# Step sizes of a state-space mixer on 96 partitions, three half blocks of the output projection moved, inputs loaded first

## The chip, the cores and the metric

The kernel runs on one core of a Trainium2 chip, in one launch. The metric is the device time of one execution in microseconds (us). TensorE (PE) multiplies, VectorE (DVE), ScalarE (ACT) and GpSimd (POOL) do the rest, SyncE (SP) and POOL issue the transfers (DMA) from and to HBM. All data is float32; a matrix product of 128 x 128 by 128 x 384 shows as two PE instructions in the trace.

## The reference, cut to what matters

One layer of a trunk over 128 context tokens and 256 latent tokens, width 2048. The layer's modulation is SiLU(cond) @ w_ada + b_ada, six columns of 2048. A mixer sub-layer projects the normed tokens by w_in and splits into two groups: a Mamba-2 state-space group (SSD, 16 heads of 64, state 128, chunks of 128 tokens, both directions) and an RWKV-7 group (16 heads of 64, both directions). Their outputs, 1024 channels each, are concatenated and go through w_out (2048 x 2048). Then 16 SwiGLU experts, each on its top tokens, and a final norm.

The step sizes of the SSD group:

```python
dt = softplus(dt_raw.reshape(b, seq, 2, 16) + dt_bias)     # 2 directions, 16 heads
A = -exp(A_log)
a_cum = cumsum(dt * A, axis=chunk)                         # within chunks of 128 tokens
decay_in = exp(where(lower, a_cum[i] - a_cum[j], -inf))    # backward direction: reversed tokens
decay_to_end = exp(a_cum[last] - a_cum)
chunk_decay = exp(a_cum[last])
y_off = (C * exp(a_cum)) @ h_in
y = y_f + reverse(y_b) + D * x
```

and at the end of the mixer `x += gate_m * (concat(y_ssd, y_rwkv) @ w_out)`.

## The kernel before

Channels lie on partitions and the 384 tokens (3 tiles of 128, the first of them the context) along the free axis. Stages follow each other, each a block in which every engine has its own list of instructions in a fixed order; engines meet by semaphores only. At the end of a block all engines wait for each other.

**setup** (lines 187 to 342). SP loads the constant table (L219), some twenty small parameter arrays as rows of 128 (L211), x in three tiles of 1 MB (L237, L239), the position table (L240), and then sixteen 1 MB pieces of w_ada through a ring of eight (L216), the narrow columns of w_in and three blocks of it. TensorE transposes the parameter rows (L270), then x (L279), then multiplies eight strips of w_ada, sums the squares for the norm, and multiplies the other eight strips (L258).

**ssd_shared** (L382 to L684) computes what all heads share. TensorE goes through sixteen more strips of w_ada (L483, ring of four) between products of w_in, then projections 3, 4 and 5 (L455), x and z of the first pair of heads (L520), B's tokens and the product of B and C (L525, L528), and last the transposes of three row arrays (L536). The raw step sizes come out of projection -1 on partitions 96 to 127; two products with slices of the identity (L460) bring both directions onto 16 partitions, one per head, with tile `dt` of 16 x 2 x 384. DVE computes the softplus by a series (L627 to L639), the running sums by a scan over 384 tokens with a reset mask (L643), their reversal for the backward direction (L647 to L653), then the four convolutions of B and C (L347 to L661) with sigmoids on ACT, the lora mixing (L671 to L674), and the product of step size and decay (L679), for which it waits for ACT's exponentials (L601 to L603). SP loads the per-head scalars A_log, dt_bias and D first of all in this block (L413 to L415).

**ssd_heads** (L687 to L945) goes over 8 pairs of heads. SP first writes the running sums, their exponentials and seven per-head values to HBM (L760), and reads them back spread over partitions: for each pair four running-sum rows onto 128 partitions each (`spread_sums`, L749), two loads of decays and two of the seven values onto 64 partitions each (`spread_decays`, L756, L757). In a turn SP issues, in this order: the z weight of the next pair (from the second turn on), the spread sums once the masks of this pair are made (`M_seg`), the x weight of the pair after once its x projection is done (L739), the final states, the next states, and the spread decays. TensorE (`body`, L801) places the 32 products of the next pair's x and z (L797, 16 each) between eight strips of w_ada (L812), which POOL loads through a ring of four (L717), and the products of the pair itself. DVE makes the masks (L907), 12 instructions of 128 x 128 from the spread sums and a column of `tokq`.

**rwkv** (L984 to L1690), 8 pairs again. In the last two pairs the free places of TensorE take products of the first half of w_out (k from 0 to 7) for output blocks 0 to 11 (L1177), which DVE adds to x (L1595). At the end stand, for the last pair, mean (L1189), centring (L1565, L1570), square, variance (L1189), root, reciprocal and scaling (L1574 to L1584). hT, the normed tokens, is last read some pairs earlier; its room is free by then.

**project_out** (L1706 to L1836) goes over 16 output blocks of 128 channels: blocks 0 to 11 with k from 8 to 15, blocks 12 to 15 with all 16 (L1770), from a ring of four weights and into three banks. DVE adds each block to x (L1825), and `done` (L1755) multiplies it by the router's weights (L1758) and transposes it (L1762). Between the blocks stand the gate columns (L1776) and the router's shift (L1782). Block n waits for the addition of block n - 3. DVE builds the router's weights (L1819, L1820) before its first addition.

**experts** (from L1843) streams the experts' weights through a ring.

## Time and profile before

| | us |
|---|---|
| median of 3 runs | 2345.91 (2338.87 to 2346.77) |
| the profiled execution | 2347.66 |
| its span | 2345.7 |
| setup, to the first work of the next stage | 70.9 |
| ssd_shared, to TensorE's first strip of the pair stage | 214.1 |
| ssd_heads, to TensorE's first RWKV product | 484.8 |
| rwkv and project_out, to TensorE's first expert-stage work | 1342.7 |
| experts, to the end | 2345.7 |

| engine | busy us | share of the span |
|---|---|---|
| PE | 2134.6 | 91% |
| PE weight load | 1072.5 | 46% |
| DVE | 854.1 | 36% |
| ACT | 399.7 | 17% |
| POOL | 156.9 | 7% |

The shares are means over stages with different limits. In a timeline a row gives the start, the time to the end of the last of its instructions, the engine, the line, and in brackets how long the engine was idle before it and what ended that. "SPq" rows are transfers as SP issues them, not their landing.

### The profile page before, as it was taken

The page shows a single profiled execution, that of the slowest core. Times are in us where ns is not written, and L with a number is a line of the kernel's source. Part 1 is how long each engine was busy: PE and PEld are TensorE (multiplying, and loading weights), DVE is VectorE, ACT ScalarE, POOL GpSimd, SP SyncE. Part 2 cuts the span into 40 slices and gives each one's busy share as a digit, 9 for nine tenths or more (in the row PEclk, how much of TensorE's full clock was granted, in tenths as well). Part 3 has the DMA queues.
Part 4 walks back from the last instruction along what each step waited for, and adds up shares of the span by engine and source line. Part 5 has one row for each costly group of instructions (what it writes and reads, how often), then busy time and mean ns, then how long its engine had stood idle before and what let it go on. Part 6 is the DMA issues. An engine that isn't in the chain of part 4 may idle for free. (4 is left out here: it accounts for less than half of the span.)

```text
span 2345.7 us, 38339 instructions
## 1 busy us (share of the span) xinstructions
PE 2134.6 (91%) x16420; PEld 1072.5 (46%) x16420; DVE 854.1 (36%) x1835; ACT 399.7 (17%) x807; POOL 156.9 (7%) x186
## 2 busy tenths in 40 slices
PE   5897999999999999999979889989988999899886
PEld 2354555446666666666655443324322432243222
DVE  1245434434566666656431131112111211122113
ACT  1123122212332233222101110001000100010002
POOL 0000111100011011101101100000000000000000
PEclk9898999999999999999989989999999999999998
DMA  9954999942211111111123399999999999999996
GB/s 368 355 167 132 316 353 339 323 128 67 52 49 43 42 52 48 43 42 40 39 76 104 124 371 413 413 414 412 413 413 413 413 413 413 413 413 413 413 413 263
DMA packets 271121, 594.03 MB, mean 253 GB/s; under 512 B 25853, under 2 KB 166231, under 8 KB 249847
## 3 DMA queue, kind: packets, MB, share of 16 engines
q1 hardware_dynamic: 253559, 524.64, 60.0%
q0 software_dynamic: 17408, 67.11, 7.5%
q8 instruction: 124, 2.03, 0.4%
q14 instruction: 30, 0.25, 0.0%
HBM read 586.89 MB, written 4.82 MB: 252 GB/s over the span
## 5 line engine op out<-in xcount | busy, mean ns | idle before, releaser
L1985 PE MATMUL bank<-w_early,picked 128*64 128x512 f32 x1024 | 242.3, 617 | 44.7 <-DMA w_early<-exp_w_up 42.6
L1184 PE MATMUL bank<-arena,w_rkv 128*128 128x384 f32 x736 | 271.7, 502 | 4.4 <-ACT raw_rkv L1408 4.4
L2164 DVE TENSOR_TENSOR x_sum<-x_sum,bank 128x512 f32<-128x512 f32 x180 | 115.4, 684 | 319.6 <-PE bank L1965 319.6
L2009 PE MATMUL bank<-arena,hid 128*64 128x512 f32 x768 | 173.5, 600 | 13.1 <-issue 11.3
L1985 PE MATMUL bank<-arena,picked 128*64 128x512 f32 x768 | 175.4, 598 | 5.2 <-DMA arena<-exp_w_up 4.8
L1184 PEld LDWEIGHTS bank<-arena,w_rkv 128*128 128x128 f32 x736 | 130.1, 189 | 89.7 <-issue 17.4
L1985 PEld LDWEIGHTS bank<-w_early,picked 128*64 128x64 f32 x1024 | 77.6, 141 | 201.2 <-issue 200.9
L797 PE MATMUL bank<-arena,w_xz 128*128 128x384 f32 x448 | 157.0, 499 | 2.6 <-DMA w_xz<-w_in 2.6
L2051 ACT COPY gu<-bank 112x512 f32<-112x512 f32 x32 | 17.2, 589 | 660.7 <-PE bank L1985 660.7
L1156 POOL TENSOR_TENSOR WI<-WX,cst 128x384 f32<-128x384 f32 x80 | 80.6, 1023 | 594.7 <-DVE WX L1613 385.7
L797 PEld LDWEIGHTS bank<-arena,w_xz 128*128 128x128 f32 x448 | 82.3, 191 | 82.3 <-issue 31.0
L1770 PE MATMUL bank<-arena,w_out_ring 128*128 128x384 f32 x320 | 108.0, 493 | 11.5 <-DMA w_out_ring<-w_out 11.5
L1985 PEld LDWEIGHTS bank<-arena,picked 128*64 128x64 f32 x768 | 54.1, 136 | 119.8 <-issue 119.4
L1965 PE MATMUL bank<-outs,G 48*128 48x512 f32 x384 | 107.0, 638 | 1.4 <-DVE outs L2183 1.4
L2009 PEld LDWEIGHTS bank<-arena,hid 128*64 128x64 f32 x768 | 60.9, 138 | 103.6 <-issue 101.6
L2183 DVE TENSOR_TENSOR outs<-bank,gates 128x512 f32<-128x512 f32 x32 | 20.6, 686 | 237.6 <-PE bank L2009 237.6
L1640 DVE TENSOR_TENSOR WI<-WI,bank 128x384 f32<-128x384 f32 x80 | 44.1, 551 | 130.4 <-PE bank L1320 85.7
L1177 PE MATMUL bank<-arena,w_rkv 128*128 128x384 f32 x192 | 76.7, 525 | 8.6 <-DVE arena L1595 8.6
L1770 PEld LDWEIGHTS bank<-arena,w_out_ring 128*128 128x128 f32 x320 | 60.5, 193 | 51.4 <-DMA w_out_ring<-w_out 12.1
L812 PE MATMUL bank<-w_ada,cond 128*32 128x512 f32 x512 | 66.1, 623 | 8.6 <-DMA w_ada<-w_ada 4.0
L1307 PEld LDWEIGHTS bank<-WI 64*64 64x64 f32 x1920 | 60.5, 136 | 27.1 <-issue 27.1
L2095 POOL TENSOR_TENSOR arena<-x_sum,gfin 128x512 f32<-128x512 f32 x4 | 5.0, 1276 | 983.6 <-DVE x_sum L2164 983.6
(405 smaller groups left out, 2732.3 us busy)
## 6 DMA issues: line engine op xcount, KB each, us to landing
arena<-exp_w_down SPq DMA_DIRECT2D x96, 1024.0 KB, 18.9
w_ada<-w_ada POOLq DMA_DIRECT2D x64, 1024.0 KB, 8.0
w_early<-exp_w_gate SPq DMA_DIRECT2D x64, 1024.0 KB, 18.6
w_early<-exp_w_up SPq DMA_DIRECT2D x64, 1024.0 KB, 18.8
arena<-exp_w_gate SPq DMA_DIRECT2D x48, 1024.0 KB, 19.0
arena<-exp_w_up SPq DMA_DIRECT2D x48, 1024.0 KB, 18.7
w_ada<-w_ada SPq DMA_DIRECT2D x32, 1024.0 KB, 11.8
w_exp<-exp_w_down SPq DMA_DIRECT2D x32, 1024.0 KB, 23.8
```

What stands on the lines that cost most here:

```text
L797: mm = pe.matmul(ps[j][:, 0:T], w[:, j, k], hT[:, k], start=(k == 0), stop=(k == KC - 1))
L812: mm = pe.matmul(ps[4][32 * j:32 * j + 32, :], cond[:, 2 * n + j // 2], wa[:, n % AR, j // 2, j % 2 * 512:(j % 2 + 1) * 512], start=(n == ...
L1156: nc.gpsimd.tensor_tensor(CT[d], W2[d][:, :, 2], m, ALU.mult).then_inc(S(f"CT_ready{d}"), 1)
L1177: mm = pe.matmul(ps[6][:, 0:T], w[:, m % 3, n % 8], mixed[:, n % 8], start=(n % 8 == 0), stop=(n % 8 == 7))
L1184: mm = pe.matmul(ps[feed_bank(i)][:, 0:T], spare[:, n] if first else w[:, m % 3, n % 8], hT[:, n % KC], start=(n % KC == 0), stop=(n % KC ...
L1307: mm = pe.matmul(ps[3 * d][HP[1 - h], c * Q:(c + 1) * Q], CT[d][HP[h], c], X[d][HP[h], c], start=True, stop=True)
L1640: ins = V.tensor_tensor(X[d], X[d], c6(ps[3 * d + 1][:, 0:T]), ALU.subtract)
L1770: mm = pe.matmul(ps[n % BANKS][:, 0:T], w[:, n % RING, k], mixed[:, k], start=(k == first(n)), stop=(k == KC - 1))
L1965: pe.matmul(ps[bank + h][:], G[rows, t * P:(t + 1) * P], outs[rows, b], start=True, stop=True).then_inc(S("add_in"), 1)
L1985: mm = pe.matmul(ps[b][COLS[j], :], picked[:, k, at:at + 64], halves[j][:, c * 1024 + b * 512:c * 1024 + (b + 1) * 512], start=(k == 0), s ...
L2009: mm = pe.matmul(ps[4 + b][COLS[j], :], hid[:, f], wd[:, n * 512:(n + 1) * 512], start=(f == 0), stop=(f == 7))
L2164: V.tensor_tensor(y, y if e else x, ps[(LAST_BANKS[i // 2 % 4] if e == LAST else 6) + i % 2][:], ALU.add).then_inc(S("added"), 1)
```

## The change

Three edits.

1. In setup, the three loads of x and the position table are issued right after the constants, ahead of the small rows.
2. In the shared stage, the step sizes lie on 96 partitions (3 tiles x 2 directions x 16 heads) by 128 tokens. Three products (one per tile) select them; every step of the series works on 96 x 128; the scan needs no reset mask; `back` marks the backward rows, for which the running sum is (a + total) - sum. The per-head scalars are loaded once per tile, after the first four pieces of w_ada. ACT's exponentials come before the convolutions, and DVE's product too. The row arrays are transposed by three products, and the per-head values (totals' exponentials and D) reach all partitions by products of ones with diagonals into tile `whole`, in place of the HBM round trip. TensorE does this ahead of x and z; B's tokens stand between x, and the halves of z. SP writes the sums and exponentials to HBM and spreads the first pair's within this stage. In HBM they lie as 96 rows of 128, so each spread copy reads three pieces (two for the decays) of 128 values.
3. The second halves of w_out's output blocks 0, 1 and 2 are loaded into hT's room at the end of the RWKV stage; seven of their eight products (k from 8 to 14) run there, around mean and variance of the last pair, and stay in banks 0 to 2. project_out does only k = 15 for them; its loads begin with block 3, and `done` of blocks 0 to 2 follows block 3.

```diff
             at = CONST["row"][0]
             sp.dma_start(cst[:], table[:, 0:at]).then_inc(S("cst_in"), 16)
+            sp.dma_start(xtok[:, 0, :], I["x_prompt"][0]).then_inc(S("x_in"), 16)
+            for t in range(2):
+                sp.dma_start(xtok[:, 1 + t, :], I["x_sample"][0, t * P:(t + 1) * P, :]).then_inc(S("x_in"), 16)
+            sp.dma_start(grid[:], table[:, at:]).then_inc(S("grid_in"), 16)
             rows_in(0, 0, I["b_ada"].rearrange("l (r c) -> (l r) c", c=P))
...
+def spread_sums(sp, S, d_cum, seg, c):
+    rows = d_cum.rearrange("(t d h) c -> h d t c", t=TILES, d=2)
+    for u in range(4):
+        h = 2 * c + u // 2
+        sp.dma_start(seg[:, u].rearrange("p (t c) -> p t c", t=TILES), rows[h:h + 1, u % 2].to_broadcast([P, TILES, P])).then_inc(S("seg_in"), 16)
+
+def spread_decays(sp, S, d_ea, eac, c):
+    rows = d_ea.rearrange("(t d h) c -> h d t c", t=TILES, d=2)
+    for h in range(2):
+        for d in range(2):
+            dst = eac[h * HD:(h + 1) * HD, d].rearrange("p (t c) -> p t c", t=2)
+            sp.dma_start(dst, rows[2 * c + h:2 * c + h + 1, d, 1:TILES].to_broadcast([HD, 2, P])).then_inc(S("eac_in"), 16)
...
+                    for t in range(TILES):
+                        rows = slice(t * 2 * HEADS, (t + 1) * 2 * HEADS)
+                        sp.dma_start(small[rows, 0:1], I["ssd_A_log"].rearrange("l d h -> (d h) l")).then_inc(S("small_in"), 16)
+                        sp.dma_start(small[rows, 1:2], I["ssd_dt_bias"].rearrange("l d h -> (d h) l")).then_inc(S("small_in"), 16)
+                    sp.dma_start(d_col[:], I["ssd_D"].rearrange("l h -> h l")).then_inc(S("small_in"), 16)
...
             for n in range(KC):
+                if n == AR:
+                    load_scalars()
...
             sp.wait_ge(S("bc_proj"), 1)
             sp.dma_start(w_xz[:, 1], w_in[:, :, 0:P]).then_inc(S("wz_loaded"), 16)
+            sp.wait_ge(S("sums_ready"), 1)
+            sp.dma_start(d_cum, cum[:, 1]).then_inc(S("rows_out"), 16)
+            sp.wait_ge(S("decay_exp"), 1)
+            sp.dma_start(d_ea, ea[:]).then_inc(S("rows_out"), 16)
+            sp.wait_ge(S("rows_out"), 32)
+            spread_sums(sp, S, d_cum, seg, 0)
+            spread_decays(sp, S, d_ea, eac, 0)
             sp.wait_ge(S("x_proj"), 1)
...
-                    if (n, k) == (3, 11):
+                    if (n, k) == (3, 6):
                         pe.wait_ge(S("dt_rows"), 1)
-                        for d in range(2):
-                            at = 96 + d * HEADS
-                            pe.matmul(ps[d][0:HEADS, 0:T], C("ident", 96, P)[:, at:at + HEADS], dtr[96:P], start=True, stop=True).then_inc(S("dt_proj"), 1)
+                        for t in range(TILES):
+                            rows = slice(t * 2 * HEADS, (t + 1) * 2 * HEADS)
+                            turned = pe.matmul(ps[0][rows, 0:P], C("ident", 96, P)[:, 96:P], dtr[96:P, t * P:(t + 1) * P], start=True, stop=True)
+                        turned.then_inc(S("dt_proj"), 1)
...
-            pe.wait_ge(S("dt_abs"), 1)
+            pe.wait_ge(S("rows_ready"), 1)
+            pe.wait_ge(S("bc_in"), 2)
+            for j, src in enumerate((dt[:], cum[:, 1], q[:, 3])):
+                pe.transpose(ps[3][:, j * ROWS:(j + 1) * ROWS], src, C("ident", 0, ROWS)[:, 0:ROWS])
+            pe.matmul(ps[3][:, 3 * ROWS:4 * ROWS], C("ones", 0, ROWS), diag[:, 0:ROWS], start=True, stop=True)
+            mm = pe.matmul(ps[3][:, 4 * ROWS:4 * ROWS + HEADS], C("ones", 0, HEADS), diag[0:HEADS, ROWS:], start=True, stop=True)
...
+            xz(0, 0, KC)
+            bc_tokens(0)
+            xz(1, 0, KC // 2)
+            bc_tokens(1)
+            xz(1, KC // 2, KC)
...
-            lora_in(0)
-            act.wait_ge(S("small_in"), 48)
-            nc.scalar.activation(small[:, 4:6], small[:, 0:2], ACT.Exp).then_inc(S("A_exp"), 1)
+            act.wait_ge(S("small_in"), 16 * (2 * TILES + 1))
+            nc.scalar.activation(small[:, 2:3], small[:, 0:1], ACT.Exp).then_inc(S("A_exp"), 1)
             act.wait_ge(S("dt_abs"), 1)
             nc.scalar.activation(q[:, 1], q[:, 1], ACT.Exp, scale=-1.0).then_inc(S("dt_exp"), 1)
+            lora_in(0)
+            act.wait_ge(S("left_ready"), 1)
+            nc.scalar.activation(ea[:], cum[:, 1], ACT.Exp)
+            nc.scalar.activation(small[:, 3:4], cum[:, 0, P - 1:P], ACT.Exp)
+            nc.scalar.activation(q[:, 2], q[:, 2], ACT.Exp).then_inc(S("decay_exp"), 1)
...
             turns(sp, body)
+            for n in range(TAIL):
+                sp.dma_start(w_tail[n], w_out[:, KC // 2:KC, n * P:(n + 1) * P]).then_inc(S("tail_loaded"), 16)
             store_states(PAIRS - 1)
...
             turns(pe, body)
+            def tail(n, k0, k1):
+                for k in range(k0, k1):
+                    pe.matmul(ps[n][:, 0:T], w_tail[n][:, k - KC // 2], mixed[:, k], start=(k == KC // 2), stop=False)
+            pe.wait_ge(S("tail_loaded"), 16 * TAIL)
+            pe.wait_ge(S("pair_done"), PAIRS - 1)
+            tail(0, 8, 10)
             mean(PAIRS - 1)
+            tail(0, 10, 13)
             variance(PAIRS - 1)
+            tail(0, 13, 15)
+            tail(1, 8, 15)
+            tail(2, 8, 15)
...
         def first(n):
-            return 0 if n >= 12 else KC // 2
+            return KC - 1 if n < TAIL else 0 if n >= 12 else KC // 2
...
-            for n in range(KC):
-                if n >= RING:
+            for n in range(TAIL, KC):
+                if n >= RING + TAIL:
                     sp.wait_ge(S("out_in"), n - RING + 1)
                 sp.dma_start(w[:, n % RING, first(n):KC], w_out[:, first(n):KC, n * P:(n + 1) * P]).then_inc(loaded[n % RING], 16)
-                if n == 1:
+                if n == TAIL:
                     sp.dma_start(rw[:], I["router_w"].rearrange("l (k p) n -> p (l k) n", p=P)).then_inc(S("rw_loaded"), 16)
...
-                if n >= 1:
-                    done(n - 1)
+                for m in range(TAIL) if n == TAIL else range(n - 1, n) if n > TAIL else ():
+                    done(m)
```

## Rows read from the trace of the kernel before

**Rows 1.** page, the span in 40 slices: GB/s moved
```profile
GB/s 368 355 167 132 316 353 339 323 128 67 52 49 43 42 52 48 43 42 40 39 76 104 124 371 413 413 414 412 413 413 413 413 413 413 413 413 413 413 413 263
```

**Rows 2.** windows at the start; columns after the engines: PEclk, DMA share, GB/s
```profile
3.00:12.00 9.00, 0.81 (x3) 0.50 (x3) 0.05 (x1) 0.00 (x0) 0.00 (x0) 1.00 0.58 195
12.00:60.00 48.00, 35.38 (x172) 14.82 (x176) 10.84 (x16) 10.29 (x19) 0.00 (x0) 0.89 1.02 416
70.00:72.00 2.00, 0.08 (x1) 0.11 (x1) 1.01 (x4) 1.04 (x3) 1.05 (x2) 0.50 1.21 291
```

**Rows 3.** timeline of PE, start to the second turn: start, us, what, idle before
```profile
19.05 4.53 PE L279 MATMUL bank<-cst,xtok 128*128 128x128 f32 x20 [7.21 <-DMA xtok<-x_sample]
107.58 1.41 PE L483 MATMUL bank<-w_ada,cond 128*32 128x512 f32 x8 [2.00 <-DMA w_ada<-w_ada]
156.44 20.80 PE L455 MATMUL bank<-arena 128*128 128x384 f32 x64
177.08 20.80 PE L520 MATMUL bank<-arena,w_xz 128*128 128x384 f32 x64
198.21 0.83 PE L528 MATMUL bank<-Cm,B 128*128 128x128 f32 x6
210.06 0.79 PE L536 MATMUL bank<-cst,dt 16*128 16x16 f32 x6 [9.23 <-DVE q L679]
214.10 3.53 PE L812 MATMUL bank<-w_ada,cond 128*32 128x512 f32 x16 [1.98 <-POOLq L102]
217.56 8.01 PE L797 MATMUL bank<-arena,w_xz 128*128 128x384 f32 x24
225.50 1.92 PE L812 MATMUL bank<-w_ada,cond 128*32 128x512 f32 x16
254.32 9.70 PE L797 MATMUL bank<-arena,w_xz 128*128 128x384 f32 x24 [2.39 <-DMA w_xz<-w_in]
```

**Rows 4.** timeline of DVE, step sizes, convolutions and first masks
```profile
153.94 1.25 DVE L627 TENSOR_SCALAR dt<-bank,small 16x384 f32<-16x384 f32 x2 [6.80 <-PE bank L460]
165.17 6.83 DVE L636 SCALAR_TENSOR_TENSOR q<-q 16x768 f32<-16x768 f32 x7
179.72 0.40 DVE L347 TENSOR_SCALAR acc<-cin,par 128x388 f32<-128x388 f32 x1
197.29 0.48 DVE L661 SCALAR_TENSOR_TENSOR Cm<-acc,par,sig 128x256 f32<-128x256 f32 x1
229.13 3.24 DVE L907 SCALAR_TENSOR_TENSOR M<-seg,tokq,cst 128x128 f32<-128x128 f32 x12 [8.08 <-DMA seg<-rows_cum]
```

**Rows 5.** one steady turn as a window; SP's timeline; landing of L739's loads
```profile
288.45:322.76 34.31, 33.95 (x180) 17.85 (x180) 14.77 (x37) 7.93 (x14) 5.71 (x8) 1.00 0.97 340
234.27 1.48 SPq L739 DMA_DIRECT2D w_xz<-w_in  x1
DMA to landing us min/median/max: 8.7/12.6/20.0
```

**Rows 6.** timeline of PE at the RWKV end and in the output projection
```profile
1195.62 0.91 PE L1189 MATMUL bank<-yc,cst 128*128 128x384 f32 x2 [0.65 <-DVE yc L1565]
1197.82 0.91 PE L1189 MATMUL bank<-gn_rstd,cst 128*128 128x384 f32 x2 [1.28 <-ACT gn_rstd L1437]
1210.21 7.33 PE L1770 MATMUL bank<-arena,w_out_ring 128*128 128x384 f32 x16 [11.48 <-DMA w_out_ring<-w_out]
1217.47 3.33 PE L1776 MATMUL bank<-cst,gcol 128*64 128x128 f32 x32
1241.87 5.33 PE L1770 MATMUL bank<-arena,w_out_ring 128*128 128x384 f32 x16
```

**Rows 7.** timeline of DVE at the same boundary
```profile
1204.20 0.56 DVE L1584 TENSOR_TENSOR arena<-yc,g 128x384 f32<-128x384 f32 x1
1206.10 0.19 DVE L1810 SCALAR_TENSOR_TENSOR gain<-modT,par 128x32 f32<-128x32 f32 x1 [1.34 <-PEq L130]
1214.23 0.42 DVE L1820 TENSOR_TENSOR rwg<-rw,gain 128x256 f32<-128x256 f32 x1
```

More of the change, by code:

```diff
@@ L411, in _, with load_scalars @@
         def _(sp):
-            with nc.allow_non_contiguous_dma(reason="per-head scalars"):
-                sp.dma_start(small[:, 0:2], I["ssd_A_log"].rearrange("l d h -> h (l d)")).then_inc(S("small_in"), 16)
-                sp.dma_start(small[:, 2:4], I["ssd_dt_bias"].rearrange("l d h -> h (l d)")).then_inc(S("small_in"), 16)
-                sp.dma_start(r7[:, 6:7], I["ssd_D"].rearrange("l h -> h l")).then_inc(S("small_in"), 16)
+            def load_scalars():
+                with nc.allow_non_contiguous_dma(reason="per-head scalars"):
+                    for t in range(TILES):
[3 more added lines that the diff above has]
+                    sp.dma_start(d_col[:], I["ssd_D"].rearrange("l h -> h l")).then_inc(S("small_in"), 16)
             def load(n):
@@ L590, in _ @@
                 lora_in(n)
+            act.wait_ge(S("lora_mixed"), 3)
+            nc.scalar.activation(lora[:, 0], lora[:, 0], ACT.Tanh)
+            nc.scalar.activation(lora[:, 2], lora[:, 2], ACT.Sigmoid)
+            nc.scalar.activation(lora[64:96, 1], lora[64:96, 1], ACT.Sigmoid)
             for g in range(2):
@@ L623, in _ @@
             dve.wait_ge(S("A_exp"), 1)
-            dve.wait_ge(S("dt_proj"), 2)
-            for d in range(2):
-                link(nc.vector.tensor_scalar(dt[:, d], ps[d][0:HEADS, 0:T], small[:, 2 + d:3 + d], None, ALU.add))
+            dve.wait_ge(S("dt_proj"), 1)
+            link(nc.vector.tensor_scalar(dt[:], ps[0][0:ROWS, 0:P], small[:, 1:2], None, ALU.add))
             nc.vector.scalar_tensor_tensor(q[:, 1], dt[:], -1.0, dt[:], ALU.mult, ALU.max).then_inc(S("dt_abs"), 1)
@@ L981, in ssd_norm, with tail_weights @@
     return scalar, tensor, vector
+TAIL = 3
+def tail_weights(rows):
+    return [rows[:, n * D + 1024:(n + 1) * D].rearrange("p (k c) -> p k c", c=P) for n in range(TAIL)]
 def rwkv(nc, I, O, table, S, sb, ps, cst, par, modT, gain, xT, C, hT, mixed, lora, spare):
@@ L1765, in _ @@
             for n in range(KC):
[L1766 removed]
+                if n >= TAIL:
+                    pe.wait_ge(loaded[n % RING], ((n - TAIL) // RING + 1) * 16)
                 if n >= BANKS:
@@ L1769, in _ @@
                 for k in range(first(n), KC):
-                    mm = pe.matmul(ps[n % BANKS][:, 0:T], w[:, n % RING, k], mixed[:, k], start=(k == first(n)), stop=(k == KC - 1))
+                    block = w_tail[n][:, k - KC // 2] if n < TAIL else w[:, n % RING, k]
+                    mm = pe.matmul(ps[n % BANKS][:, 0:T], block, mixed[:, k], start=(n >= TAIL and k == first(n)), stop=(k == KC - 1))
                 mm.then_inc(S("out_in"), 1)
```

157 lines of the change are left out of this document (68 added, 89 removed).

## The prediction

> **What bounds the kernel now.** I read the page's slices first, then the chain of waits, then windows and timelines of the stages that the diff touches. In the slices DMA moves a flat 413 GB/s from some 1350 us to the end [rows 1]: the experts wait for their weights, their loads begin when their stage begins, and nothing in them is edited. So whatever the stages before gain should reach the end undiminished. Four places lie in the way of the change.
>
> Start: after the constants land, DMA moves 195 GB/s over 3 to 12 us, then 416 GB/s up to 60 us [rows 2]. SP spends those 9 us issuing small row loads, with the megabytes of x queued behind them. From 12 us on the queue is never empty: TensorE's stall at 105.6 to 107.6 us is a wait for such a load [rows 3].
>
> Shared stage: TensorE is dense to about 201 us, idles 9.23 us for DVE's last product, transposes, and begins the pair stage at 214.10 [rows 3]. The delay is DVE's queue: the step sizes start at 153.94 on 16 partitions, the four convolutions run from 179.72 to 197.77 [rows 4] (197.29 + 0.48), the lora mixing, an exponential and the product follow.
>
> Pair stage: TensorE bounds a steady turn, 33.95 of 34.31 us, with DMA at 0.97 [rows 5]. The second turn is longer, because an x weight came 2.39 us late and the slow clock made the first twelve products 9.70 instead of 8.01 us [rows 3]: 4.1 us together. That load was issued at 234.27 [rows 5], after the pair's masks, which had waited 8.08 us for the spread running sums [rows 4].
>
> RWKV tail: while one chain of ACT and DVE finishes the last pair, TensorE idles 0.65, 1.28 and 11.48 us, 13.4 in all, and the first output block then takes 7.33 us where a warm one takes 5.33 [rows 6].
>
> **x first.** The bytes stay the same, only their place moves. The 9 us at 195 GB/s would run at 416: 9 x (416 - 195) / 416 = 4.8 us of transfer moved into the hole. The small rows now lie behind 4.6 MB and land near 15 us instead of 11, but x is transposed behind them and was there only at 19.05 [rows 3], so TensorE's transposes still start 3 us sooner, and the loads of w_ada, which pace everything up to 42 us and again SP's last issues of that stage, come 4.8 us sooner. DVE's chain at the stage's end hangs on the same loads. I take 4.8 (ends 2.5 and 5). The per-head scalars are seven loads instead of three, with 208 four-byte pieces instead of 80, now behind four w_ada loads. They stand ahead of the load on which TensorE stalls at 107 us. Nothing of before shows their price alone: between nothing and 1 us, I take 0.2 lost.
>
> **Step sizes on 96 partitions.** A DVE step on 16 x 768 costs 0.98 us (6.83 / 7), one on 128 x 128 0.27 us (3.24 / 12) [rows 4]. Some twenty steps go from about 0.9 to 0.3, the reciprocal with them, and two short exponentials stay between: the rows are ready near 163 us (9 us after 153.94) where the convolutions alone began at 179.72. The convolutions then end near 163 + 18 = 181. TensorE wants the rows at 177.1 and the convolved B at 188, so DVE leaves the path, with 14 and 7 us to spare. What is late next is TensorE itself: from 156.44 come 20.64 us (two projections), five short transposes and products (1.0, by the 0.79 of six instructions), the same 20.64 for x and z, two groups of B tokens at 1.3 each (0.83 for the products, about 0.45 for the transposes) [rows 3]. That ends at 201.3, less 0.65 since the step sizes' selection now streams 3 x 128 instead of 2 x 384 columns (0.65 us per 384 [rows 6]): 200.7. SP still issues the next z load then, 0.4, and the stage boundary costs 1.3 (DVE's 1.34 in [rows 7]): the first turn starts at 202.4 instead of 214.10. Gain 11.7 (ends 8, if DVE or ACT keeps a tail of 3 to 4 us, and 12.5). SP issues the spreads at about 165 and waits meanwhile only for things that are early; behind it queue the weights of pair 1, which need x's projection at 188 anyway.
>
> The first strips took 3.53 us cold against 1.92 [rows 3]. The idle before them falls from 13 us to 1.7, and the granted clock fell after idle of 2.39 us [rows 3]: I take half of the 1.6 us, 0.8.
>
> **Rows spread early.** The 8.08 us that the first masks waited lay beside a busy TensorE and are worth nothing in themselves. But the next x weight is then issued when the feed of x is done, 16 us into the turn and not 20 (234.27 - 214.10), and it was 2.39 late: the stall goes with its slow clock, 4.1 us (ends 0 and 4.1).
>
> Against this, each pair's running sums come from rows of 128: 1536 packets of 512 bytes where there were 512 of 1536, and the decays double their 256 packets; two tiny loads of 64 packets go. SP issues eight spreads a pair as before. Loads in 512-byte packets moved 291 GB/s, long rows 416 [rows 2]: for 1.05 MB this makes at most 3.6 - 2.5 = 1.1 us of transfer a turn, in a turn of 34.3 us that TensorE fills. I take 0.5 lost over the whole stage (ends 0.5 gained, by the removed loads, and 7.7, all of it exposed in seven turns). The Trainium skill's page DMA: Bandwidth & Descriptors (Specifications) calls 512 bytes enough for line rate; by it this cost is nothing and the sum 0.5 us better. The trace disagrees, and the trace decides.
>
> **Three half blocks in the tail.** 21 of 160 products of 0.65 us leave the projection and run in the idle: 13.7 us of work. In before's times: the last y product ends at 1194.97; two products push the mean from 1195.62 to 1196.27; three more behind it (1.95) push the variance to 1198.9, 1.05 later than 1197.82. DVE then ends at 1204.76 + 1.05 = 1205.8 [rows 7], but TensorE has 0.65 + 16 x 0.65 to do and ends at 1209.9: it is late next, by 4 us. Boundary 1.4: 1211.3. One product, a wait for the gate columns (DVE needs 1.0 us, 0.35 of wait), their transposes 3.3 [rows 6], two products: 1216.9. Block 3 then waits for DVE's first addition, which stands behind the router's weights: ready at 1214.65 [rows 7], 8.6 us into the stage, now 1.8 sooner since one 512 KB load less lies ahead (a half of 3.6 us at 291 GB/s), so 1218.1, and with the addition 1218.9: 2.0 us idle. New idle 1.4 + 0.35 + 2.0 = 3.75. Gone: from 1194.97 to 1210.21 less 1.3 of mean and variance, 13.9, and 2.0 of slow clock. I leave 0.8 for a clock that may fall once more: 13.9 + 2.0 - 3.75 - 0.8 = 11.4 (ends 8.5, if the router comes no sooner and the clock falls twice, and 13). The tail's loads go out after SP's last weight, some 35 us before they are wanted, on idle queues.
>
> **Sum.** 4.8 - 0.2 + 11.7 + 0.8 + 4.1 - 0.5 + 11.4 = 32.1 us. The profiled execution took 2347.66, so 2315.6; it lies 1.75 above the median of the three timed runs, and I say 2315.
>
> **Rivals.**
> (1) The start gives little: the rows land late enough behind x that TensorE, not the loads, paces the first stage. The saturated queue from 12 us on speaks against it. 2315.6 + 4 = 2320.
> (2) The tail gives half: the mean and variance behind foreign products, a cold clock at the boundary and the router wait take 5 to 6 us more. That TensorE is already last there by 4 us speaks for it, that the idle is three times as long against it. 2321.
> (3) The finer packets are all exposed and the second turn's stall stays: 7.2 + 4.1 later, 2327. DMA at 0.97 speaks for it; 0.36 us of idle TensorE in a steady turn against it.
> (4) Slower than before: the pair stage becomes bound by SP's loads. The spreads share DMA with the long packets of w_ada, and if each short packet waits its turn behind one of those, a weight load lands not 12.6 but 20.0 us after its issue, as one did [rows 5]. The z weight is issued at the start of a turn and wanted 14.5 us in (strips 1.9 twice, feed 8.0, four products of 0.65 [rows 3]), so what the landing grows by beyond 1.9 us is waiting; the median leaves next to nothing of that once SP's four spreads ahead of it are counted, so it would come up to 7.4 us late, with 1.7 of slow clock: 9.1 x 7 = 64 us, 2379. It decides from 4.6 us a turn: 2.9 of waiting and 1.7 of slow clock. The same page (Queues, rings and completion order) has the engines take queues in turn packet by packet, which is how this would come about; that 512-byte weight loads already run there in time is against it.
> (5) The step sizes don't leave the path, since ACT's new order (scalars' exponential ahead of the lora copy) holds back projection 4 or the convolutions: 2 to 6 us less, 2319.
>
> **How the numbers follow.** Forecast 0.55, (1) 0.12, (2) 0.12, (3) 0.08, (4) 0.02, (5) 0.11. Own range of the forecast 2310 to 2321. Further gain is bounded by 12.5 + 13 + 5 + 4.1 + 1.6 = 36.2, 2311.5, less 4 for runs as low as the lowest shown. Range 2307 to 2326. What a measurement can tell from no change is 0.5%, 11.7 us. All cases but (4) and a meeting of (2) and (3) with each other pass it: faster 0.95, same 0.03, slower 0.02.
>
> **What would show it.** 400 GB/s or more over 3 to 12 us and x's transposes near 15.8; the pair stage's first strip 16 us earlier than 214.10; no DVE wait for the spread sums and no wait for a weight in the second turn; steady turns still 34.3; in the tail TensorE dense to its end, and about 2 us idle ahead of output block 3. Steady turns of 35 us or more, or an idle of 5 us ahead of block 3, would make the prediction wrong.

## The result, and the profile after

The changed kernel takes 2407.15 us (median of 4 runs, 2405.19 to 2413.23) where the kernel before, in the same session, took 2346.34 (4 runs): a ratio of 1.0281, 95% interval 1.0261 to 1.0301. Forecast were 2315 and "faster". The profiled execution took 2405.4 us with a span of 2403.4, that is 57.7 us more than the span before.

Three of the four parts did about what was forecast; one cost about three times what all of them gained. The page's slices show where. Each is 60 us long (58.6 us before):

```profile
GB/s 373 363 147 189 228 252 235 229 266 133 72 51 47 42 41 51 47 51 32 49 53 91 149 248 402 413 413 413 413 413 413 413 413 413 413 413 413 413 413 261
```

Against [rows 1], slices 5 to 8, the pair stage, moved 316 to 353 GB/s and now move 228 to 252, and the stage reaches into a ninth. The whole stage as one window, from its first strip to the first product of the RWKV stage, after:

```profile
198.57:559.93 361.36, 284.37 (x1369) 138.52 (x1369) 118.27 (x296) 69.07 (x117) 42.95 (x60) 0.86 0.77 241
```

and before (columns after the span: PE, PEld, DVE, ACT, POOL busy with instructions, PEclk, DMA share, GB/s):

```profile
214.10:484.79 270.69, 256.43 (x1368) 132.79 (x1369) 118.07 (x296) 63.43 (x113) 42.81 (x60) 0.97 0.94 322
```

It is 90.7 us longer, with TensorE's instructions the same: 62.7 us more idle (361.36 - 284.37 against 270.69 - 256.43) and 27.9 us more busy, since the granted clock fell from 0.97 to 0.86 in a TensorE that idles so often. Read the last two columns together: the DMA engines are called busy for 0.77 of the time but move 241 GB/s; at the ratio of before they would have moved 264. So a small part of the loss lies inside the packets, and the larger part is time in which the engines show as idle. The stage's DMA bytes did not rise (241 GB/s over 361.36 us and 322 over 270.69 are both 87 MB).

TensorE's timeline shows what it waits for, at the places of [rows 3]:

```profile
198.57 1.92 PE L842 MATMUL bank<-w_ada,cond 128*32 128x512 f32 x16 [1.55 <-POOLq L102]
200.43 8.01 PE L827 MATMUL bank<-arena,w_xz 128*128 128x384 f32 x24
...
252.59 9.74 PE L827 MATMUL bank<-arena,w_xz 128*128 128x384 f32 x24 [11.89 <-DMA w_xz<-w_in]
281.94 1.94 PE L842 MATMUL bank<-w_ada,cond 128*32 128x512 f32 x8 [4.50 <-DMA w_ada<-w_ada]
```

The first strip comes at 198.57 instead of 214.10, and warm (1.92 us, not 3.53). Then it waits, 11.89 us at one place, for both kinds of weights. And SP's own timeline shows the queue that carries one of them:

```profile
165.20 1.97 SPq L369 DMA_DIRECT2D seg<-rows_cum  x4
167.21 10.47 SPq L378 DMA_DIRECT2D eac<-rows_ea  x4
...
210.43 2.41 SPq L369 DMA_DIRECT2D seg<-rows_cum  x4
213.10 4.92 SPq L788 DMA_DIRECT2D w_xz<-w_in  x1
219.86 23.42 SPq L808 DMA_DIRECT2D out_ssd_fwd<-fin  x1
...
249.03 0.59 SPq L788 DMA_DIRECT2D w_xz<-w_in  x1
```

The x weight that TensorE got at 252.59 had been issued at 213.10, right behind four spreads, and so landed 39.4 us later. The store behind it took 23.42 us for its issue alone, with those spreads still in the queue, and the z weight behind the store was issued at 249.03, 10 us after the turn that needs it had begun (at 238.77). The landing times of these weights (8.7/12.6/20.0 in [rows 5]) are now

```profile
DMA to landing us min/median/max: 10.1/21.7/39.4
```

and those of the sums' spreads, first before, then after:

```profile
DMA to landing us min/median/max: 3.3/4.6/11.4
```

```profile
DMA to landing us min/median/max: 7.2/16.3/30.5
```

The most telling view is of a place where nothing competes: the first pair's spreads are now issued in the shared stage, with DMA otherwise idle. A window there (its last two numbers are again DMA share and GB/s):

```profile
168.00:170.00 2.00, 2.00 (x7) 1.14 (x6) 1.89 (x5) 0.27 (x1) 0.00 (x0) 1.00 0.17 44
```

44 GB/s from engines busy 0.17 of the time. Packets of 512 bytes at 44 GB/s are one every 11.6 ns for all sixteen engines together, whose loads of 512-byte pieces moved 291 GB/s [rows 2]. The experiments are about that number.

### The profile page after: what moved, and what is told of

It is laid out like the page before. It is cut to its first block and busy times, and to the rows that moved or that the text cites. A ratio compares the mean times of both kernels' runs of the same rounds, so it can differ in the third digit from the quotient of the medians.

```text
span 2403.4 us, 38367 instructions
## 1 busy us (share of the span) xinstructions
PE 2145.1 (89%) x16411; PEld 1071.2 (45%) x16411; DVE 837.0 (35%) x1839; ACT 402.5 (17%) x810; POOL 157.5 (7%) x186
## 5 line engine op out<-in xcount | busy, mean ns | idle before, releaser
L827 PE MATMUL bank<-arena,w_xz 128*128 128x384 f32 x448 | 168.9, 527 | 31.7 <-DMA w_xz<-w_in 31.7
L827 PEld LDWEIGHTS bank<-arena,w_xz 128*128 128x128 f32 x448 | 87.2, 203 | 122.0 <-issue 39.6
L842 PE MATMUL bank<-w_ada,cond 128*32 128x512 f32 x512 | 79.9, 724 | 42.6 <-DMA w_ada<-w_ada 39.5
L1830 PE MATMUL bank<-arena,w_out_ring 128*128 128x384 f32 x272 | 90.0, 486 | 1.8 <-DVE arena L1885 1.8
L1349 PE MATMUL bank<-WI 64*64 64x64 f32 x1920 | 66.1, 220 | 4.2 <-issue 4.2
## 6 DMA issues: line engine op xcount, KB each, us to landing
w_ada<-w_ada POOLq DMA_DIRECT2D x64, 1024.0 KB, 12.6
w_exp<-exp_w_down SPq DMA_DIRECT2D x32, 1024.0 KB, 23.8
```

The lines of the kernel that those rows point to most:

```text
L827: mm = pe.matmul(ps[j][:, 0:T], w[:, j, k], hT[:, k], start=(k == 0), stop=(k == KC - 1))
L842: mm = pe.matmul(ps[4][32 * j:32 * j + 32, :], cond[:, 2 * n + j // 2], wa[:, n % AR, j // 2, j % 2 * 512:(j % 2 + 1) * 512], start=(n == ...
L1349: mm = pe.matmul(ps[3 * d][HP[1 - h], c * Q:(c + 1) * Q], CT[d][HP[h], c], X[d][HP[h], c], start=True, stop=True)
L1830: mm = pe.matmul(ps[n % BANKS][:, 0:T], block, mixed[:, k], start=(n >= TAIL and k == first(n)), stop=(k == KC - 1))
```

## The experiments

I had two theories for it. A: each packet of a spread has a price of some 11.5 ns, whatever its size. D: the pieces share a supply, since the three tiles of a row lie exactly 16 KB apart. And there was the question whether the pieces alone do the damage.

**Whole rows back (whole_rows).** The edit, in the changed kernel:

```
-        d_cum, d_ea = (nc.dram_tensor(n, (ROWS, P), ...
+        d_cum, d_ea = (nc.dram_tensor(n, (HEADS, 2, T), ...
-        sp.dma_start(seg[:, u].rearrange(...), rows[h:h + 1, u % 2].to_broadcast([P, TILES, P]))
+        sp.dma_start(seg[:, u], d_cum[h:h + 1, u % 2].to_broadcast([P, T]))
```

> The changed kernel with one thing put back: the running sums and decays lie in HBM as one row of 384 per head and direction (twelve writes in place of two, since a partition now holds a tile of 128), and are spread in packets of 1536 and 1024 bytes by 6 loads a pair, as before the change. Nothing else differs. Theory A (the cost of the change is the spreads, each of whose packets costs SP's queue about the same 11 to 12 ns whatever its size, so that 2048 packets a pair hold it for 23 us and 896 for 10): the waits for w_xz and w_ada of the pair stage (74 us in all) go, and the time is 2346 - 15 (setup and shared stage, as the trace of after shows them) - about 11 (tail, forecast) - 4 (the second turn's stall) = 2316 us, between 2311 and 2322. Rival B (the pair stage is slow because the spreads of the first pair now stand ahead in SP's queue and because h0, x and z loads keep another order, not because of the pieces): stays above 2390. Rival C (the tail or the RWKV stage lost something too): lands between, 2325 to 2350.

Measured 2312.02 us, ratio to before 0.9867 (0.9850 to 0.9883). The same window of its trace, and its pair stage:

```profile
168.00:170.00 2.00, 2.00 (x8) 1.21 (x7) 1.89 (x5) 0.39 (x2) 0.00 (x0) 1.00 0.81 232
...
198.72:464.36 265.64, 253.50 (x1369) 131.81 (x1369) 118.16 (x296) 69.09 (x117) 42.97 (x60) 0.99 0.95 328
```

232 GB/s where there were 44, and a stage of 265.6 us. The layout of the rows costs the changed kernel 95 us (medians of two sessions; by the ratios to before it is 97), and B, the order of the loads, and C, a loss in other stages, are out.

**The pieces alone, in the kernel before (before_pieces).**

```
-   ("rows_cum", (HEADS, 2, T)), ("rows_ea", (HEADS, 2, T))
+   ("rows_cum", (TILES * 2 * HEADS, P)), ("rows_ea", (TILES * 2 * HEADS, P))
-   sp.dma_start(seg[:, u], d_cum[h:h + 1, u % 2].to_broadcast([P, T]))
+   sp.dma_start(seg[:, u].rearrange(...), in_rows(d_cum)[h:h + 1, u % 2].to_broadcast([P, TILES, P]))
```

> The kernel before with one thing of the change added: the rows in HBM cut by tile, so that a pair's spreads are 1536 packets of 512 bytes for the sums and 512 of 512 bytes for the decays (896 packets in all before: 512 of 1536, 256 of 1024 and 128 of 28 bytes, which stay here); thirteen writes of rows in place of three. Step sizes, x and tail are as before. Theory A: the pair stage of before, 270.7 us long, grows by what it grew in the changed kernel, about 75 to 90 us, so 2420 to 2440. Rival B (order, not pieces): 2346 to 2352. A part cost only (the pieces matter only together with the earlier start): 2355 to 2400.

2463.4 us, 1.0507 (1.0483 to 1.0532): 120 us over before, more than in the changed kernel, where it was 95. Here the 128 packets of 28 bytes a pair are still in the queue and the first pair's spreads fall into the stage itself; which of it makes the 25 us was not taken apart. Theory A had said 75 to 90.

**Another distance (padded).**

```
-        d_cum, d_ea = (nc.dram_tensor(n, (ROWS, P), ...
+        d_cum, d_ea = (nc.dram_tensor(n, (TILES, 2 * HEADS * P + 1088), ...
```

> The changed kernel, still in pieces of 512 bytes (2048 packets a pair), but the three tiles of a row in HBM lie 20.4 KB apart at an odd pitch (5184 elements) in place of exactly 16 KB, with six writes of rows in place of two. Theory A (a price for each packet): no change, 2400 to 2412. Rival D (the three pieces fall on the same part of the memory because they lie 16 KB apart, and each part gives about 45 GB/s): most of the loss goes, 2320 to 2345.

2325.24 (2 runs), 0.9921. The same 2048 packets a pair, 82 us gone: theory A falls. Its window shows 121 GB/s, about three times 44 and three is the number of pieces:

```profile
168.00:170.00 2.00, 2.00 (x8) 1.18 (x7) 1.89 (x4) 0.00 (x0) 0.00 (x0) 1.00 0.52 121
```

**Other rows (distinct).**

```
-    rows = d_cum.rearrange("(t d h) c -> h d t c", t=TILES, d=2)
-        ... rows[h:h + 1, u % 2].to_broadcast([P, TILES, P])
+    x = x_prompt[0].rearrange("r (a b c) -> r a b c", b=4, c=P)
+        ... x[:, 0:TILES, u]
```

> The changed kernel, but the spreads read distinct rows of x_prompt, partition p its own row, in the same 2048 packets of 512 bytes with the same destinations, in place of one row repeated for all partitions; and the masks take their per-token scalar from the step sizes instead of the negative sums. So running sums and decays are left out of the result: same instructions, other numbers. Theory A in its plain form (each packet of 512 bytes costs the queue 11 to 12 ns wherever it reads): no change, 2400 to 2412. Rival E (what is slow is that 128 packets read the same 512 bytes one after another): the spreads move at the 291 GB/s of the 512-byte loads of w_in or better, some 3.6 us a pair, and the time is that of whole rows or below, 2308 to 2322.

2312.87 (2 runs), 0.9868, and 236 GB/s in that window. So 512-byte packets are no trouble when every partition reads its own. In this kernel it took both: one row repeated, and a distance of 16 KB.

**Spreads by themselves (spreads_alone, spreads_more, spreads_turns).** One queue, nothing else running, each pattern waited for.

```
+ for name, steps, width in PATTERNS:
+     for u in range(copies):
+         sp.dma_start(dst[:, u], AP(exp_w_up, offset=n * 1M, ap=steps + [[1, width]])).then_inc(S("got"), 16)
+     sp.wait_ge(S("got"), ...)
```

> Spreads by themselves: the whole of the reference's computation is left out, no engine but SP does anything, and its time stands for nothing. Nineteen patterns follow each other, each of four loads (two of the long ones) of 192 KB to 128 partitions, each waited for before the next is issued: one row for all partitions, as 1536 bytes in one piece; as three pieces of 512 bytes 16, 32, 8, 4, 2 and 1 KB apart, 16.5, 17 and 20.25 KB apart, and 0 apart; as six of 256 bytes 16 KB and 0.5 KB apart; as two of 1024 bytes, one of 2048 and 4096; and rows of each partition's own, end to end, 16 KB and 16.5 KB apart. Theory D (pieces on the same part of memory share one supply of some 45 GB/s, whoever reads them): 1536 bytes in one piece 200 GB/s or more, pieces 16, 32 and 8 KB apart 45, 20.25 KB apart 130, and own rows 16 KB apart as slow as the repeated row. Rival E (it is repetition of one row that is slow): own rows fast at any distance, pitches all alike. Theory A (a price for each packet, 11.5 ns): 1536 bytes 133 GB/s, 512 bytes 45 at every pitch, 256 bytes 22, 4096 bytes 356.

The windows go from a pattern's first packet to the end of its last (columns: POOL busy, PEclk, DMA share, GB/s). The twelve lines are, in this order: (1) one row as 1536 bytes; (2) to (7) three pieces of 512 bytes 16, 32, 8, 4, 2 KB and 16.5 KB apart; (8) three pieces at the same address; (9) six of 256 bytes 16 KB apart; (10) one row as 4096 bytes; (11) each partition's own rows end to end, which go as packets of 1536 bytes, and (12) own pieces of 512 bytes, the partitions 16 KB apart:

```profile
9.53:16.04 6.51, 0.00 (x0) 1.00 0.53 121
17.38:37.27 19.89, 0.00 (x0) 1.00 0.39 40
38.80:57.80 19.00, 0.00 (x0) 1.00 0.13 41
59.12:78.65 19.53, 0.00 (x0) 1.00 0.35 40
79.99:94.38 14.39, 0.00 (x0) 1.00 0.30 55
95.71:103.13 7.42, 0.00 (x0) 1.00 0.45 106
113.03:120.82 7.79, 0.00 (x0) 1.00 0.81 101
138.55:158.28 19.73, 0.00 (x0) 1.00 0.26 40
159.70:198.52 38.82, 0.00 (x0) 1.00 0.08 20
230.03:233.76 3.73, 0.00 (x0) 1.00 0.69 281
235.03:238.44 3.41, 0.00 (x0) 1.00 0.73 230
239.83:243.15 3.32, 0.00 (x0) 1.00 0.80 237
```

Divide by packets. Pieces 8, 16 or 32 KB apart: 1536 packets in 19.0 to 19.9 us, 12.4 to 12.9 ns each, exactly as slow as three reads of one address. Half the size, twice the packets: 12.6 ns again. One row as 1536 bytes: 512 packets in 6.51, 12.7 ns too. Pieces 2 or 16.5 KB apart: little more than a third of the time. Pieces 4 KB apart, of which the first and third are 8 KB apart: three quarters. Two patterns not printed above fit less closely: two pieces of 1024 bytes 16 KB apart took 14.8 ns a packet (15.16 us for 1024), and the one row of 1536 bytes took 13.2 and 14.2 ns in the two later runs. Even the row of 4096 bytes went at 14.6 ns a packet (3.73 us for 256), and at 16.4 (249 GB/s) in the run after. So packets that read the same place wait for each other, some 12.4 to 14.8 ns each, whatever they carry up to 1536 bytes; and two addresses a multiple of 8 KB apart, at these small distances, are the same place. Own rows 16 KB apart are fast, which theory D had wrong: it is not a supply of bytes, and 128 different rows are not caught by it. Where it was right (8, 16, 32 KB alike, 20.25 free with 109 GB/s) it was right for the wrong reason. Its 200 GB/s for one row of 1536 bytes was wrong as well: 121. The 232 GB/s of whole rows in the kernel do not contradict this 121. Here all four loads read the same row; there the four loads of a pair read four rows, 1.5 KB apart.

The DMA shares say one thing more. Lines (2), (3), (4) and (8) have the same 40 or 41 GB/s at shares of 0.39, 0.13, 0.35 and 0.26: while such packets wait for each other, the engines show as idle for most of the time, and how much of the wait shows as busy differs.

> Spreads by themselves again, the whole of the reference's computation left out, its time stands for nothing. Eight loads of one 512-byte row to 128 partitions; one row of 1536, 2048 and 4096 bytes; three pieces 64 KB, 256 KB, 1 MB and 8.5 KB apart; eight loads in which the partitions share 2, 4, 8, 16 and 32 rows of 512 bytes that lie 16 KB apart; the same with 2, 4 and 16 rows 512 bytes apart; rows of each partition's own 16, 8 and 64 KB apart. If a place is the address within 8 KB and nothing else (places): three pieces 64 KB to 1 MB apart as slow as 16 KB apart (21 us), 2 to 32 rows by 16 KB as slow as one row (13 us for eight loads), and 2, 4 rows by 512 bytes 2 and 4 times as fast. But own rows 16 KB apart were fast, so higher address bits must count too: then from some number of rows, or some distance, on it gets fast; this run is to find which. If it is repetition of a row that counts, 2 to 32 rows by 16 KB get faster in proportion.

(1) to (3) three pieces 64 KB, 256 KB and 1 MB apart; then eight loads (1024 packets) in which blocks of partitions share (4) to (6) 2, 8 and 16 rows 16 KB apart, and (7), (8) 2 and 4 rows 512 bytes apart:

```profile
42.98:55.11 12.13, 0.00 (x0) 1.00 0.33 65
56.44:63.29 6.85, 0.00 (x0) 1.00 0.45 115
64.63:72.18 7.55, 0.00 (x0) 1.00 0.54 104
82.02:95.68 13.66, 0.00 (x0) 1.00 0.13 38
113.11:125.84 12.73, 0.00 (x0) 1.00 0.37 41
127.54:133.87 6.33, 0.00 (x0) 1.00 0.47 83
143.35:155.45 12.10, 0.00 (x0) 1.00 0.15 44
157.12:163.24 6.12, 0.00 (x0) 1.00 0.28 86
```

At 256 KB and 1 MB three pieces are free of each other; 64 KB is between. Eight rows 16 KB apart (41 GB/s) are no faster than one row (40 in this run); 16 are twice as fast. Higher address bits count, then, but I can't say how.

The lines with 2 and 4 rows measure something else. In the trace the semaphore by which a load reports its landing comes up in 16 steps for most patterns, but in 3 steps in lines (4) and (7), in 5 in line (8) and in 9 in line (5), always one more than the count of the source's outermost step, which is 2, 4 and 8 there. And in line (7) two or three packets are under way at any moment, in line (8) four to six. So these loads ran on two, four and eight of the sixteen engines, which is read from these counts, as the profile names no engine. Two engines gave 44 GB/s and four 86, some 22 each; lines (7) and (8) show that, and nothing about places, and line (4) could not have shown more than 44 either. Line (5), with eight engines and 41 GB/s, is slow by its place.

> Spreads by themselves a third time, the whole computation left out, its time stands for nothing. Each pattern is eight loads of one 512-byte piece to 128 partitions (1024 packets), but neighbouring partitions now take different rows in turn: 2, 4, 16 and 64 rows 16 KB apart, 2, 4 and 16 rows 512 bytes apart, 2 and 4 rows 2 KB apart; beside them halves of the partitions on 2 rows 2 KB apart, one row for all, and a row for each. In the run before this one halves and quarters by 16 KB were as slow as one row (38 GB/s), and so were halves 512 bytes apart (44), while quarters 512 bytes apart had 86. If a place is the address within 8 KB as long as it is one of few rows: turns by 16 KB stay at 38 to 44 up to 4 rows; turns of 2 and 4 rows by 2 KB give 80 and 160. If the halves by 512 were slow because all engines work on one half at a time, turns of 2 by 512 give 80 and halves by 2 KB stay at 40; if they were slow because 0 and 512 bytes are one place, turns of 2 by 512 stay at 40 and halves by 2 KB give 80.

Here neighbouring partitions take turns: (1) to (4) 2, 4, 16 and 64 rows 16 KB apart; (5), (6) 2 and 4 rows 512 bytes apart; last, two halves of the partitions on two rows 2 KB apart:

```profile
24.94:39.28 14.34, 0.00 (x0) 1.00 0.31 37
41.03:54.39 13.36, 0.00 (x0) 1.00 0.28 39
56.16:62.76 6.60, 0.00 (x0) 1.00 0.29 79
64.47:77.06 12.59, 0.00 (x0) 1.00 0.14 42
78.74:86.37 7.63, 0.00 (x0) 1.00 0.46 69
88.00:93.14 5.14, 0.00 (x0) 1.00 0.35 102
...
118.56:130.67 12.11, 0.00 (x0) 1.00 0.14 43
```

In turns, two rows 512 bytes apart give 69 GB/s, where one row gave 39, both with 16 steps of the semaphore. So 0 and 512 are two places. Turns of 2 and 4 rows 16 KB apart, 16 steps too, stay at 37 and 39, so they are slow by their place. In halves, even rows 2 KB apart give 43, and 64 rows 16 KB apart in turns give 42; the outermost step of both counts 2, the semaphore comes up in 3 steps, and two engines give no more. The expectation was that halves would be slow because all engines work on one half at a time; by these counts the halves are slow because only two engines work at all. So the 42 of 64 rows is no sign that their addresses collide; 16 rows in turns (79, on eight engines) were not at that limit. How far down a place goes, why 4 rows stop at 102, and which distances collide from 64 KB on stays open: the rule holds for few rows and small distances, which is the kernel's case.

**The rule tried in the kernel (skewed).** One number in the changed kernel, 18 rows of room for 16 (the rows are then written in twelve pieces and not in two):

```
-        d_cum, d_ea = (nc.dram_tensor(n, (ROWS, P), ...
+        d_cum, d_ea = (nc.dram_tensor(n, (2 * TILES, 18 * P), ...
```

> The changed kernel in its own pieces of 512 bytes (2048 packets a pair), with one number changed: a block of 16 heads' rows takes 18 rows in HBM instead of 16, so that two directions lie 9 KB apart and two tiles 18 KB, where it was 8 and 16. (Twelve writes of rows take the place of two, since the blocks no longer join.) The theory that the spreads alone left standing: packets that repeat a place wait for each other, some 12.4 ns each, and addresses 8, 16 and 32 KB apart count as one place, so that a load's three pieces, and both directions, shared one; 9 and 18 KB apart they are places of their own (a pair's twelve rows then fall on twelve). It expects the time of own rows and of whole rows, 2309 to 2315, and seg's landing near 3.4 us where the changed kernel has 16.3. If the run padded (2325) was as good as 512-byte pieces get, 2320 to 2328. If packet size alone counts, 2400.

2316.58 us (6 runs), 0.9887 (0.9867 to 0.9906), 90.6 us under the changed kernel; in its quiet window 297 GB/s at its best:

```profile
168.00:170.00 2.00, 2.00 (x8) 1.21 (x7) 1.90 (x4) 0.00 (x0) 0.00 (x0) 1.00 1.01 297
```

That is 1.6 us above what was expected at most, and seg lands after a median of 5.0 us, not 3.4. The interval overlaps that of whole_rows; whether 512-byte packets still cost some 4 us here was not told apart.

**The other parts, each alone.** x first, in the kernel before (the four issues moved ahead of the rows, as in the diff):

```
+            sp.dma_start(xtok[:, 0, :], I["x_prompt"][0]) ...   # ahead of rows_in(0, 0, ...)
```

> The kernel before with x's three loads and the position table issued ahead of the small rows, and nothing else of the change. The forecast's own term was 4.8 us (transposes of x 3 us sooner, the loads of w_ada 4.8 sooner). The trace of the changed kernel says 3.1 us at the end of the first stage, because the rows landed at 18.54 us and the transposes of x began at 19.15, no sooner than before. Rival: the rows, now behind x, hold the transposes and take all back, 0. So 2339 to 2340 by the forecast, 2340 to 2341.5 by the trace, 2343 by the rival; the ratio to before between 0.9975 and 1.000.

2338.89 (12 runs), 0.9981 (0.9968 to 0.9994): a gain of 4.4 us with an interval of 1.4 to 7.5. And taken out of whole_rows:

> The changed kernel with rows of 384 in HBM (packets of 1536 and 1024 bytes, as in the run whole_rows, 2312.0), and x loaded last again, as before the change. If loading x first is worth what it takes off the end of the first stage, 3.1 us, this is 2315; by the forecast's 4.8 it is 2317; if what it gains comes back as a longer wait for w_ada in the shared stage (1.98 us there with x first), 2312 to 2313.

2313.89 (5 runs), 1.9 us above whole_rows, each against the same kernel before but in different sessions. Loading x first is worth 2 to 4 us; the runs don't say it closer.

The tail, in the kernel before (the diff's part from `turns(sp, body)` on):

```
+            for n in range(TAIL):
+                sp.dma_start(w_tail[n], w_out[:, KC // 2:KC, n * P:(n + 1) * P])
```

> The kernel before with the three half blocks of w_out in the RWKV tail, and nothing else of the change. The forecast's term is 11.4 us, 2332. In the changed kernel's trace the stretch from the last y product to the end of the projection is 133.8 us against 146.0 before: 12.1 us, 2331. Rival: the stages after take part of it back, since the experts' first weights are loaded from the moment the projection begins and not from its end: 6 us or less, 2337 or more.

2329.19 (6 runs), 0.9945 (0.9929 to 0.9962): 12.9 us by the ratio.

The shared stage, with whole rows, x last and the old tail:

```
-   dt = sb(st, "dt", [HEADS, 2, T])
+   dt = sb(st, "dt", [ROWS, P])        # and the rest of that part; rows in HBM (HEADS, 2, T)
```

> The change without two of its parts and with rows of 384 in HBM: step sizes on 96 partitions and spreads issued in the shared stage, but x loaded last and the tail of before. The forecast's terms for what is left are 11.7 + 0.8 + 4.1 - 0.2, 16.4 us: 2326. By subtraction from the runs so far: whole_rows_xlast 2313.9 without the tail's 13.6 (before_tail against before): 2327.5. If the tail's gain and this one's overlap, less than that, 2324.

2327.81 (6 runs), 0.9933 (0.9914 to 0.9951): 15.7 us by the ratio, where 16.4 were forecast. The three parts add up to 4.4 + 12.9 + 15.7 = 33.0 us; together, with whole rows, they give 31.2 (0.0133 of 2343.3). Nothing shows that they get in each other's way; the intervals, some 3 to 4 us on each part, leave room for a few us.

## Why the prediction was wrong, point by point

**The step that failed** is the cost term of "Rows spread early": "I take 0.5 lost over the whole stage (ends 0.5 gained, by the removed loads, and 7.7, all of it exposed in seven turns)". Measured: 95.7 us, the 361.36 us of the pair stage against 265.64 with whole rows. The term priced the spreads by loads of the same packet size, 291 GB/s [rows 2]. But those loads read a different row for each partition. A spread reads one row 128 times, and the quiet window shows 44 GB/s. Its transfer is then 1.05 MB / 44 GB/s = 24 us a turn in place of 3.6, in a turn of 34.3 whose DMA was full before [rows 5]. The upper end of 7.7 stood on the same row and so bounded nothing. The row it should have stood on was in the trace: the spreads of before themselves. Around their issue at 216 us, this view of before has

```profile
216.00:219.00 3.00, 3.00 (x17) 0.92 (x8) 1.83 (x3) 0.76 (x1) 1.43 (x2) 0.77 0.60 102
```

102 GB/s, a beginning load of w_ada included, for packets of 1536 bytes that the sum took at 416. That gap of four should have been asked about. It is not the spreads' price alone: in the quiet window of whole_rows the same packets of 1536 bytes moved 232 GB/s. But even that is little more than half of what the sum took.

The text set the Trainium skill's page DMA: Bandwidth & Descriptors (Specifications), 512 bytes are enough for line rate, against the 291 GB/s of the loads, and chose the latter. Neither spoke of repeated reads: own rows in 512-byte packets had 237 GB/s here, one repeated row 40.

**Rival (4)**, slower because the pair stage is bound by SP's loads, came true and had 0.02. Its place and its sign were right, weight loads that land late, and its 64 us were nearer than the forecast. Its mechanism was not: short packets were to wait behind the long ones of w_ada, but they crawl with nothing beside them. What it left out was the store held for 23.42 us, and w_ada on POOL's queue, whose landing rose from a median of 8.0 to 12.6 us (8.5 with whole rows). How the spreads delay that other queue stays open. From 278 to 282 us POOL's loads moved 1.38 MB, 345 GB/s, beside 0.17 MB of SP's; but of the loads issued at 264.00 and 265.02 nothing had moved by 268, with the engines busy for 0.64 of the time on SP's packets, and from 268 to 276 they moved 0.74 MB with the engines mostly idle.

**x first**: 195 GB/s over 3 to 12 us became 417, as forecast:

```profile
3.00:12.00 9.00, 0.00 (x0) 0.00 (x0) 0.00 (x0) 0.00 (x0) 0.00 (x0) 1.00 1.00 417
12.00:60.00 48.00, 37.46 (x199) 16.85 (x203) 13.12 (x20) 10.29 (x19) 0.00 (x0) 0.93 1.00 384
...
18.54 0.81 PE L270 MATMUL bank<-cst,rows 128*128 128x128 f32 x3 [18.54 <-DMA rows<-rwkv_mu]
19.15 5.43 PE L279 MATMUL bank<-cst,xtok 128*128 128x128 f32 x24
```

But the small rows took their slowness with them: from 12 to 18 us 325 GB/s moved where there were 425, which is 1.4 us, and the rows came at 18.54 us, not 15. (The rest of the step from 416 to 384 GB/s is the window's last 4 us, into which the short rows of w_narrow have moved.) The transposes of x began where they had, at 19.15, and not 3 us sooner as the term's reasoning had them. The next stage started 3.1 us sooner (68.79 for 71.92), not 4.8; that is the term's lower region (its ends were 2.5 and 5).

**Step sizes**: the stage took 15.5 us less to the first strip, 3.1 of it from the start, so 12.4 where 11.7 were forecast (11.5 with the scalars' 0.2). The convolutions started at 159.41, not 163, and DVE ended them at 177.48, not 181. The masks met no wait. The forecast of what is late next, TensorE itself, held. First strip and second turn: with whole rows the pair stage is 5.05 us shorter than before (0.8 + 4.1 - 0.5 = 4.4 forecast), but only part of that came about as argued. The stall in the second turn, which was to go, is still there in whole_rows, 2.16 us in place of 2.39:

```profile
237.11 8.01 PE L830 MATMUL bank<-arena,w_xz 128*128 128x384 f32 x24 [2.16 <-DMA w_xz<-w_in]
```

The x weight was issued 14.5 us into the first turn (213.25) and not 20, but it took 23.8 us to land where it had taken 20. What went is the slow clock behind the wait: 8.01 us for 9.70. That turn gains 1.9 of the forecast 4.1; the first strips gain 1.6 and not 0.8, and the remaining 1.5 lie in two later turns that no term named. That the total is near is luck.

**Tail**: from the last y product to the end of the projection 133.8 us where there were 146.0; 12.1 gained, 11.4 forecast. TensorE after, at [rows 6]'s places:

```profile
1268.57 10.48 PE L1442 MATMUL bank<-arena 128*128 128x384 f32 x32
1280.37 0.88 PE L1830 MATMUL bank<-arena 128*128 128x384 f32 x2 [1.31 <-PEq L130]
1281.41 3.33 PE L1836 MATMUL bank<-cst,gcol 128*64 128x128 f32 x32 [0.16 <-DVE gcol L1872]
...
1288.01 5.40 PE L1830 MATMUL bank<-arena,w_out_ring 128*128 128x384 f32 x16 [1.78 <-DVE arena L1885]
```

The idle of 11.48 is gone; the new ones, 1.31, 0.16 and 1.78, were forecast as 1.4, 0.35 and 2.0. The 0.8 us left for a slow clock were not needed.

The sum closes: -15.5 to the first strip, +90.7 in the pair stage, -12.1 in the tail, +0.8 behind it, and -6.1 in the RWKV stage (704.1 us for 710.2), which nobody had forecast: same instructions, the granted clock 1.00 for 0.99, and whole_rows has 5.0 of it as well (705.2 us); its cause was not tried. That makes 57.8, with rounding, for the 57.7 measured. With the one term replaced the time is near the forecast, 2312.0 with whole rows for 2315 predicted, but not by the terms alone: the 5.0 us of the RWKV stage are in it, which no term foresaw, and without them it would be 2317. That kernel is the one to keep: it beats before by 1.3% and the changed kernel by 95 us.

## What to carry to other kernels

Before a layout in HBM is cut for the benefit of the engine that writes it, price its readers by their own rows: GB/s of these very loads, in a stretch where nothing competes. A load that gives one row to all partitions is bound by how often it touches a place, not by its bytes, so keep the row long and in one piece, and do not put its pieces 8, 16 or 32 KB apart. And a bound taken from an operation that differs in one property, here whose row is read, is no bound.

## What the runs showed of the hardware that was not expected

Packets that read one place in HBM follow each other at 12.4 to 14.8 ns, counted over the whole core, for 256, 512, 1024 and 1536 bytes alike (spreads_alone, spreads_more and spreads_turns): 20 GB/s with 256 bytes, 40 with 512, up to 121 with 1536; one row as 4096 bytes had 281 and 249 in two runs. Pieces 8, 16 and 32 KB apart count as one place, 2, 16.5, 256 KB and 1 MB apart as several. Most of the wait does not show as busy engines: 40 or 41 GB/s went with DMA shares from 0.13 to 0.39, so a low share does not mean that the queue is free. A queue that holds such packets holds what stands behind them, 23.42 us for the issue of one store. Loads whose source has an outermost step that counts 2 or 4 ran on two or four engines, by the 3 and 5 steps of their semaphores, and had 42 to 44 and 86 GB/s.
